# Where the mask of chosen keys is added in a prompt's attention: on TensorE by an identity product, or on VectorE in PSUM

## What is computed

```python
def sparse_attend(q, k_sel, v_sel, valid):
    s = jnp.einsum('bqkgd,bqskd->bqkgs', qg, k_sel) * (HEAD_DIM ** -0.5)
    s = jnp.where(valid[:, :, None, None, :], s, -jnp.inf)
    p = jax.nn.softmax(s, axis=-1)
    o = jnp.einsum('bqkgs,bqskd->bqkgd', p, v_sel)
    ...
def block(i):                                  # queries 128 i to 128 i + 127
    sc = indexer_scores(qib, wib, ki)
    sc = jnp.where((key_pos[None, :] <= qpos[:, None])[None], sc, -jnp.inf)
    _, idx = lax.top_k(sc, topk)
    valid = idx <= qpos[None, :, None]
    return sparse_attend(qb, _gather_rows(k, idx), _gather_rows(v, idx), valid)
```

## Time and profile before

| | us |
|---|---|
| median of three runs | 2375.65 |
| lowest, highest | 2374.2, 2377.28 |
| the profiled execution | 2376.64 |
| span of its trace | 2374.8 |
| TensorE products busy | 2289.6 (96%) |
| TensorE weight loads busy | 2196.8 (93%) |
| VectorE busy | 1819.2 (77%) |
| ScalarE busy | 1001.1 (42%) |
| GpSimd busy | 501.9 (21%) |

### The profile page before, as it was taken

How to read it: one execution, slowest core, us unless ns; L and a number is a source line. 1 busy time by engine, 2 the same in 40 slices (tenths; PEclk the granted TensorE clock), 3 DMA queues, 4 the chain that set the end, 5 groups by cost and what they waited for, 6 DMA issues and landing times.

```text
span 2374.8 us, 48270 instructions
## 1 busy us (share of the span) xinstructions
PE 2289.6 (96%) x17572; PEld 2196.8 (93%) x17572; DVE 1819.2 (77%) x2617; ACT 1001.1 (42%) x1441; POOL 501.9 (21%) x534
## 2 busy tenths in 40 slices
PE   7999999999989998999999999999999989999898
PEld 7977999998758997999999999999999989999898
DVE  5688999997624548877777777777777887888897
ACT  6154344333532224444444444444444553443444
POOL 2324899650560101010100101001010110000000
PEclk9999999999999999999999999999999999999999
DMA  7414232322695453443444434444344683544543
GB/s 261 120 34 120 74 85 80 93 72 87 200 319 151 130 147 97 126 120 106 136 125 122 121 106 136 125 122 124 104 135 117 170 246 87 153 134 135 151 107 103
DMA packets 455456, 307.43 MB, mean 129 GB/s; under 512 B 23275, under 2 KB 436451, under 8 KB 454656
## 3 DMA queue, kind: packets, MB, share of 16 engines
q1 hardware_dynamic: 441376, 272.27, 40.4%
q0 software_dynamic: 13968, 33.68, 4.9%
HBM read 269.56 MB, written 37.18 MB: 129 GB/s over the span
## 4 chain that ended last, share of the span: by engine, by line
PE 80%; DVE 6%; issue 5%; POOL 3%; ACT 3%; DMA 1%; SPq 1%; DVEq 0%; POOLq 0%; ACTq 0%
PE ps L2472 54%; PE ps L2094 10%; PE ps L2109 5%; POOL y L760 3%; PE ps L2113 3%; PE ps L2383 1%; PE ps L2213 1%; PE ps L2357 1%; ACT opH L1162 1%; PE ps L2230 1%; DVE wr L1860 1%; PE ps L2403 1%; ACT tap L991 1%; DVE opH L1886 1%; PE ps L2339 1%
## 5 line engine op out<-in xcount | busy, mean ns | idle before, releaser
L2472 PE MATMUL ps<-opX,wp 128*128 128x272 f32 x7392 | 935.2, 289 | 10.0 <-DVE t L1925 5.5
L2472 PEld LDWEIGHTS ps<-opX,wp 128*128 128x128 f32 x7392 | 934.1, 189 | 10.7 <-DVE t L1925 5.7
L2472 PE MATMUL ps<-opH,wh 128*128 128x272 f32 x2464 | 470.3, 291 | 28.2 <-DVE h L2009 19.3
L1836 DVE TENSOR_TENSOR wp<-wr,wp 128x1024 fp32r<-128x1024 f32 x264 | 319.4, 1224 | 188.8 <-ACT wp L1145 186.3
L2472 PEld LDWEIGHTS ps<-opH,wh 128*128 128x128 f32 x2464 | 390.4, 190 | 32.9 <-DVE h L2009 21.9
L2094 PE MATMUL ps<-xs,whi 128*128 128x272 f32 (+1 forms) x2368 | 397.3, 289 | 4.8 <-POOL wlo L750 2.3
L2472 PE MATMUL ps<-opH,wl 128*128 128x272 f32 x1232 | 356.9, 290 | 0.0
L1145 ACT CAST wp<-wr 128x1024 fp32r<-128x1024 f32 x264 | 273.6, 1053 | 174.1 <-DVE wr L1829 139.2
L2094 PEld LDWEIGHTS ps<-xs,whi 128*128 128x128 f32 (+1 forms) x2368 | 335.7, 188 | 7.7 <-issue 2.3
L2094 PE MATMUL ps<-xs,wlo 128*128 128x272 f32 (+1 forms) x1184 | 245.1, 288 | 0.0
L1156 ACT CAST wh<-wr 128x768 fp32r<-128x768 f32 (+1 forms) x192 | 150.0, 782 | 215.3 <-PE ps L2472 149.4
(11 more groups left out here) (338 smaller groups left out, 2670.6 us busy)
## 6 DMA issues: line engine op xcount, KB each, us to landing
wr<-in_w_gate SPq DMA_DIRECT2D x88, 512.0 KB, 4.7
wr<-in_w_up SPq DMA_DIRECT2D x88, 512.0 KB, 7.0
raw<-in_w_in SPq DMA_DIRECT2D x72, 512.0 KB, 3.8
wr<-in_w_down SPq DMA_DIRECT2D x96, 384.0 KB, 5.4
rawH<-hid_dram SPq DMA_DIRECT2D x21, 816.0 KB, 7.0
raw<-in_w_out SPq DMA_DIRECT2D x32, 512.0 KB, 5.2
hid_dram<-hid SPq DMA_DIRECT2D x88, 136.0 KB, 1.8
hid_dram<-td SPq DMA_DIRECT2D x66, 136.0 KB, 1.8
```

Of the source, the lines that this page charges most:

```text
L1836: ve.tensor_tensor(w[:, 1, :, :], src[:, :, :], w[:, 0, :, :].bitcast(F32), ALU.subtract).then_inc(s_wlo, 1)
L2472: ins = te.matmul(prod_bank(par, i), w[:, t, :], op[:, x, t, :], start=(i in (0, 1, 3) and t == 0 and w is whi_ and x == 0), stop=(t == kk ...
```

## The change

VectorE adds the mask to the scores in PSUM, in place (new line 1720), and waits for that before the maximum. TensorE no longer multiplies the mask by the identity; its scores' product starts the bank's sum itself. Waits and counts between the engines stay as they were.

```diff
--- before.py
+++ after.py
@@ -1716,7 +1716,9 @@
                     dve.wait_ge(s_s, x + 1)
                     if x >= 4:
                         dve.wait_ge(s_p, x - 3)
-                    ve.reduce_max(stat[:, 36 + x % 4:37 + x % 4], ps[:, (0, 1, 4, 5)[x % 4], 0:w], AX.X
+                    b0, bank = BO[block_head(x)[0]], (0, 1, 4, 5)[x % 4]
+                    ch.link(ve.tensor_tensor(ps[:, bank, 0:w], ps[:, bank, 0:w], biasP[:, b0:b0 + w], ALU.add))
+                    ve.reduce_max(stat[:, 36 + x % 4:37 + x % 4], ps[:, bank, 0:w], AX.X
                                   ).then_inc(s_nm2, 1)
                     dve.wait_ge(s_nm2, x + 1)
                     ve.tensor_scalar(stat[:, 24 + x % 4:25 + x % 4], stat[:, 36 + x % 4:37 + x % 4], -ASCALE, None,
@@ -2335,9 +2337,8 @@
                     bank = (0, 1, 4, 5)[x % 4]
                     if x >= 4:
                         pe.wait_ge(s_p, x - 3)
-                    te.matmul(ps[:, bank, 0:w], identb[:, :], biasP[:, BO[i]:BO[i] + w], start=True, stop=False)
                     te.matmul(ps[:, bank, 0:w], qT[:, hh, P * i:P * i + P], kT[:, hh // GRP, 0:w],
-                              start=False, stop=True).then_inc(s_s, 1)
+                              start=True, stop=True).then_inc(s_s, 1)
                 if 0 <= x - 2 < 32:
                     z = x - 2
                     pe.wait_ge(s_pn, z + 1)
```

## The result

The changed kernel takes 2388.05 us as a median of five runs (2385.63 to 2390.61), the one before 2377.28 in the five runs beside it. The ratio is 1.0043, with a 95% interval of 1.0032 to 1.0055: 7.6 to 13.1 us slower. The forecast was 2385.6, slower.

A forecast was written before the change was run, and what follows sets the result against it. VectorE was taken to set the pace in heads 4 to 11, TensorE in the 512-wide groups. Group growths summed to +10.0 us on the profiled 2376.64, giving 2386.6, as a median 2385.6; range 2379.5 to 2394.

The forecast's parts named there:

- The price of the addition: VectorE's added pass costs 0.34, 0.48, 0.61 and 0.75 us by width; with its wait, 18.4 us over 32 heads.
- rival 3: VectorE's mixed-type additions run at half the price, 0.2 to 0.4 us: +1.5 us, 2377.2; chance 0.06.
- The wait on its own result: On VectorE, a waited pair pays full duration plus 0.03 us, while unwaited neighbours overlap by 0.09.
- Rival 2: VectorE's wait on its own result is free, an addition occupying 0.66 us at 512 columns: +6.5 us, 2382.1; chance 0.13.
- Group by group: Growth of the prompt's attention stage by groups of heads, from heads 0 to 3 through head 31: +10.0 us in sum.
- paced by VectorE alone: In heads 4 to 11 VectorE sets the pace, busy 6.81 of 7.16 and 7.06 of 7.78 us.
- On the path in the 512-wide groups only: TensorE's identity product, 4.3 us in all, lies on the path only in heads 12 to 15 and 28 to 31.
- VectorE's remaining wait: VectorE's wait for scores falls from 11.3 us to 3 or less, more than half of it in the 512-wide groups.
- no cushion: Behind the stage, the DMA-full stretch from 671 to 708 us takes in none of the 10 us.
- rival 4: TensorE's clock falls in the stage; ten us at the lower level add 4 us, 2389.6; chance 0.15.
- the ring: Two-head loop through TensorE, VectorE and ScalarE: 4.94 us at 512 columns with the addition, 4.16 without.

The follow-up runs named there:

- the spread subtractions: Kernel before with line 1733's eight subtractions moved from steps 3 to 10 to steps 3, 6 to 24: stage 62.47 us against 62.13, ratio 1.0000.
- the stage of 86.57 us: Changed kernel with a second, waited-for addition of the mask behind the first, executed once: stage 86.57 us against 70.78.
- the fused kernel: No identity product; one VectorE instruction adds the mask and takes the maximum: stage 60.79 and 60.47 us, ratio to the kernel before 0.9992 and 1.0007.
- the second measurement (10.7): The changed kernel measured once more against the kernel before: 2388.62 us, ratio 1.0047, 10.7 us slower, stage 70.82 us.

## Why the prediction was right

1. **The place and the sign: right.** Product off TensorE, addition on VectorE, one stage, a loss. Both parts were seen apart: +10.4 to 11.1 and -1.8 to -2.4 us.
2. **The price of the addition: 8% too high.** I took 0.746 us from line 1510, the nearest form that writes PSUM. It is 0.692, and with the result in SBUF it is 0.690. So the maximum and line 1739 were the right neighbours, and bfloat16 for the second operand cost or gained nothing (rival 3 is out). With its wait it is 0.33, 0.47, 0.60 and 0.73 us, 17.0 us in all and not 18.4.
3. **The wait on its own result: right,** 0.11 to 0.12 us measured against 0.12. Rival 2, the free wait, is out.
4. **Group by group.** Expected +0.65, 2.0, 2.2, 1.15, 0.3, 1.15, 0.95, 0.75, 0.8; measured, window by window, +0.68, 1.71, 1.78, 1.23, 0.46, 0.77, 0.83, 0.46, 0.72. The sum is 8.65 and not 10.0. The lower price accounts for at most 18.4 - 17.0 = 1.4 us, if all of it was on the path, which is as much as the difference. It doesn't account for the single groups: heads 8 to 11 and 20 to 23 came out 0.4 lower, more than the 0.2 that four cheaper additions give, and heads 12 to 15 and 16 to 19 came out higher, so errors cancelled in the sum. That heads 4 to 11 of the kernel before were paced by VectorE alone was wrong, as the spread subtractions show: line 1733 out of the way left heads 8 to 11 where they were. They were near enough to VectorE's limit that the addition still came on top with 1.71 of its 1.8 us in heads 4 to 7 and 1.78 of 2.4 in heads 8 to 11.
5. **The product.** "On the path in the 512-wide groups only" was too narrow: these groups gave 0.42 and 0.43 us of the 2.4, and the rest came in pieces of 0.2 to 0.4 us from the narrower ones, heads 4 to 7 excepted. Beside the addition it was worth 1.8 us. The forecast took no separate term for it, so what it missed is inside the groups of item 4.
6. **VectorE's remaining wait** is 4.2 us, not 3 or less, and 2.9 of it is in the 128-wide groups, 0.8 in the 512-wide ones, where more than half was expected.
7. **What is behind: no cushion, right; the equal lengths, luck.** From the stage's end to the last product of the pages' stage (the product of the new tokens' values, line 2437) it is 80.97 us before and 81.47 after, and 81.53 behind the stage of 86.57 us, so a stage 24 us longer is not taken in there. Over all runs it is 80.5 to 82.2. The whole stretch behind the stage is 1740.2 to 1748.1 us, and it differs by 4.7 us between the two executions of the fused kernel and by 2.5 between those of the changed one, mostly in the output projection (194.4 to 196.3 us up to line 2472's start) and in the down-projection (499.7 to 505.1). The changed kernel's 1742.88 has the shorter output projection (194.61 against 196.24) and the longer end of the last section; these cancelled.
8. **The sum and the time.** The stage grew by 1.35 us less than forecast, the median by 0.8 us more (10.8). So the time came closer than the working deserves: an error in the stage was made up by something outside it. One microsecond of that is the last section's. The other microsecond, which the second measurement (10.7) shows again, is unexplained, though both intervals reach down far enough to hold it.
9. **The clock (rival 4)** fell no more than before: 0.92 and 0.87 in the first two windows against 0.92 and 0.83. Its price showed in other kernels: 0.7 us for a dip in heads 20 to 23, and 0.28 us in heads 4 to 7 of the fused kernel, a group in which the prediction has the lower clock hide behind VectorE.

## What to carry to other kernels

Before you move an elementwise step from one engine to another, write down the ring, head by head, that each engine closes; an engine that waited 11 us of 57 for its input took in only 6 to 7 of 17 new ones, since a second pass over the scores sits in series between product and exponential. Count one pass over PSUM at the price of the maximum, plus 0.11 to 0.12 us for each wait of the engine on its own result. If a mask must go to VectorE, join it with the pass that is there: one instruction that adds and takes the maximum gave back 10 us of the stage.

## What the runs showed of the hardware that was not expected

The length of the kernel's end goes with the product's being there, far from its place. From the start of the last product of line 2472 (hidden times down-projection) to the end of the span it is 18.3 to 18.4 us in the traces of all six kernels that have the products with the identity and 19.3 to 19.4 us in all eight traces of kernels that don't. In the last wait, that of SP for the landing of out_y_sample (us in total, times, longest), the kernel before shows

```profile
SPq L131 <- DMA out_y_sample<-yo: 2.3, 1, 2.3
```

and the changed one

```profile
SPq L131 <- DMA out_y_sample<-yo: 3.1, 1, 3.1
```

and so do the others (2.2 to 2.3 us with the products, 3.0 to 3.3 without); that is most of the difference. The code there is the same. It is about 1.05 us of the 10.8, and the fused kernel loses it from its 1.3 to 1.7. Why a DMA's landing should depend on 32 matrix instructions 1700 us earlier stays open, and no run was made for it. The two sets of kernels also differ in the number of TensorE's instructions, which no run here tells apart from the products themselves.

One VectorE pass that adds a bfloat16 tile to a PSUM bank in place and takes the row's maximum runs at the speed of either alone, 0.70 us for 512 columns, with 0.14 us to read the maximum.
